# Expert weights of a mixture-of-experts layer: loads of 32 KB per partition, and the activations' transposition on VectorE

## What is computed

```python
    a = jnp.einsum('td,edf->tef', t, w_gate)      # 32 experts, w_gate and w_up (32, 2048, 512)
    u = jnp.einsum('td,edf->tef', t, w_up)
    act = jax.nn.silu(a) * u * combine[:, :, None]
    y = jnp.einsum('tef,efd->td', act, w_down)    # w_down (32, 512, 2048)
```

## Time and profile before

| what | value |
|---|---|
| time, median of 3 runs | 1390.5 us (1388.91 to 1390.74) |
| span of the profiled execution | 1388.4 us |
| PE busy | 1117.8 us, 81% |
| DVE, ACT busy | 545.0 us, 331.1 us |
| DMA, all queues | 481.20 MB, mean 347 GB/s |
| HBM read | 478.52 MB |

### The profile page before, as it was taken

One profiled execution on the slowest core, in us unless ns is written; L12 is line 12 of the kernel. 1 busy time (PEld: TensorE's weight loads), 2 busy tenths in 40 slices (PEclk: granted clock), 3 DMA queues, 4 the chain that ended last, 5 costly groups with the idle time before them and its releaser, 6 DMA issues.

```text
span 1388.4 us, 21683 instructions
## 1 busy us (share of the span) xinstructions
PE 1117.8 (81%) x8748; PEld 638.7 (46%) x8748; DVE 545.0 (39%) x1151; ACT 331.1 (24%) x611; POOL 33.2 (2%) x96
## 2 busy tenths in 40 slices
PE   8999999999999988677766667676766766767766
PEld 7888887878888633222222223222222222222222
DVE  5545576566665633332232232223232232222323
ACT  5654456665554210000000000000000000000002
POOL 1000000110001000000000000000000000000001
PEclk9999999999999999988998889888889998889898
DMA  7866653226785999999999999999999999999997
GB/s 241 274 200 182 177 170 109 92 92 226 271 291 172 410 423 426 428 425 425 427 426 427 426 425 426 428 426 426 427 424 426 427 429 425 427 424 427 428 424 306
DMA packets 93623, 481.20 MB, mean 347 GB/s; under 512 B 11719, under 2 KB 22093, under 8 KB 61454
## 3 DMA queue, kind: packets, MB, share of 16 engines
q1 hardware_dynamic: 93084, 478.22, 86.4%
q10 hardware_dynamic: 306, 2.11, 0.4%
q0 software_dynamic: 192, 0.31, 0.1%
HBM read 478.52 MB, written 2.10 MB: 346 GB/s over the span
## 4 chain that ended last, share of the span: by engine, by line
PE 47%; DMA 40%; ACT 5%; SPq 4%; DVE 3%; issue 2%; ACTq 0%; DVEq 0%
DMA gu<-in_w_up 40%; PE ps L588 7%; PE ps L590 7%; PE ps L589 7%; PE ps L1038 7%; PE ps L1093 5%; PE ps L1012 4%; SPq L424 3%; DVE w_lo L1603 1%; PE ps L1023 1%; SPq L434 1%; PE ps L555 1%; ACT x_slots L1509 1%; PE ps L816 1%; PE ps L818 1%
## 5 line engine op out<-in xcount | busy, mean ns | idle before, releaser
L1038 PE MATMUL ps<-gu,xe 128*32 128x256 f32 x3968 | 301.8, 471 | 178.1 <-DMA gu<-in_w_up 178.1
L1038 PEld LDWEIGHTS ps<-gu,xe 128*32 128x32 f32 x3968 | 148.7, 134 | 351.1 <-DMA gu<-in_w_up 222.8
L2109 DVE TENSOR_TENSOR x_sum<-ps,x_sum 128x512 f32<-128x512 f32 x240 | 149.1, 684 | 325.4 <-PE ps L1050 325.4
L1603 DVE TENSOR_TENSOR w_lo<-w_raw,w_hi 128x1024 fp32r<-128x1024 f32 (+1 forms) x137 | 163.2, 1200 | 129.2 <-ACT w_hi L1213 126.1
L588 PE MATMUL ps<-w_hi,a_hi 128*128 128x512 f32 (+1 forms) x468 | 183.0, 391 | 0.0
L589 PE MATMUL ps<-w_lo,a_hi 128*128 128x512 f32 (+1 forms) x468 | 179.8, 384 | 0.0
L590 PE MATMUL ps<-w_hi,a_lo 128*128 128x512 f32 (+1 forms) x460 | 176.9, 385 | 0.0
L1213 ACT ACTIVATE w_hi<-w_raw 128x1024 fp32r<-128x1024 f32 (+1 forms) x137 | 141.1, 1039 | 129.3 <-PE ps L590 114.7
L1093 PE MATMUL ps<-down,turned 128*32 128x512 f32 x976 | 119.5, 633 | 24.4 <-ACT turned L1522 24.4
L1516 ACT ACTIVATE sg<-ps 128x128 f32<-128x128 f32 x31 | 8.6, 278 | 546.0 <-PE ps L1038 546.0
L1012 PE MATMUL ps<-x_res,hot 128*32 128x512 f32 x496 | 111.9, 1030 | 0.0
(11 more groups left out here) (337 smaller groups left out, 884.1 us busy)
## 6 DMA issues: line engine op xcount, KB each, us to landing
gu<-in_w_gate SPq DMA_DIRECT2D x60, 2048.0 KB, 29.7
gu<-in_w_up SPq DMA_DIRECT2D x59, 2048.0 KB, 34.3
down<-in_w_down SPq DMA_DIRECT2D x118, 1024.0 KB, 20.9
w_raw<-in_w_in SPq DMA_DIRECT2D x56, 512.0 KB, 3.8
w_raw<-in_w_out SPq DMA_DIRECT2D x32, 512.0 KB, 4.7
w_raw<-in_w_mem_kv SPq DMA_DIRECT2D x16, 512.0 KB, 4.1
down<-in_w_down SPq DMA_DIRECT2D x16, 512.0 KB, 11.8
gu<-in_w_up SPq DMA_DIRECT2D x7, 1024.0 KB, 12.7
```

The lines of the kernel that those rows point to most:

```text
L1038: mm = pe.matmul(ps[5][j * SLOTS:(j + 1) * SLOTS, 0:2 * P].rearrange("s (m f) -> s m f", m=2), xe[:, k, :], gu[side][:, b, :, kk, j * P:(j ...
L1603: ve.tensor_tensor(w_lo[:, u % RING, :, 0:n], w_raw[:, u % RING, :, 0:n], w_hi[:, u % RING, :, 0:n], ALU.subtract).then_inc(S("w_split"), 1)
L2109: ins = ve.tensor_tensor(x_sum[:, t, cols], ps[g][:, :], (x_res if first else x_sum)[:, t, cols], ALU.add)
```

## The change

Gate and up of an expert are each loaded by one DMA of 4 MB, a run of 32 KB for each partition, into `gu` laid out as gate or up, then all 16 slices. Down is one tile `down` of 32 KB a partition, loaded by one DMA of 4 MB: partition p holds rows 4p to 4p + 3 of the expert's down weights, which lie behind each other in HBM. `load_gate_up` waits once, for `gu_used1`; `load_down` waits once, for `down_used`, which PE counts up after the last matmul of `project_down`. PE waits once for all of an expert's gate and up before the first matmul of `gate_up`, and once for all of its down weights.

As the hidden features are now spread over partitions in fours, DVE writes `act` with the four features of a partition set 32 columns apart, and turns it with one transposition in blocks of 32 by 32 (`gate(n)`); PE's transposition of `act` and ACT's copy of it are gone, and `project_down` waits for `act_turned`. DVE waits for `down_used` of the expert before, since `act_t` is overwritten. `x_sum` and `down_first` move to the place of `down0`, and `down` takes the place of the old `x_sum` and `down1`.

At the start, expert 0's down weights all come early, and where its last rows came (L467) now comes the first half of expert 1's in one DMA of 2 MB with runs of 16 KB. Expert 3's gate is issued ahead of expert 2's down, its up behind it. The pieces of experts 0, 1 and 2 and those of the last expert keep their sizes.

```diff
-        gu = [place("gu0", [P, 2, 2, KD // 2, FE], offset=e_at),
-              place("gu1", [P, 2, 2, KD // 2, FE], offset=w_at)]
-        down0 = place("down0", [P, 2, D], offset=e_at + 4 * 16 * 1024)
-        down1 = place("down1", [P, 2, D], offset=a_lo_at)
+        gu = [place("gu0", [P, 2, KD, FE], offset=e_at),
+              place("gu1", [P, 2, KD, FE], offset=w_at)]
+        down = place("down", [P, NJ, D], offset=a_hi_at)
+        at[0] = max(at[0], e_at + 5 * 16 * 1024)
-        turned_6 = place("turned_6", [P, TT + 1, P], offset=mla_mask_at)
+        comb_t = place("comb_t", [P, TT, P], offset=mla_mask_at)
+        act_t = place("act_t", [P, P], offset=mla_mask_at + 1024)
-        comb_t, act_t = turned_6[:, 0:TT, :], turned_6[:, TT, :]
-
-        x_sum = place("x_sum", [P, TT, D], offset=a_hi_at)
-        down_first = place("down_first", [P, 2, D], offset=a_hi_at)
+        x_sum = place("x_sum", [P, TT, D], offset=e_at + 64 * 1024)
+        down_first = place("down_first", [P, 2, D], offset=e_at + 64 * 1024)
...
 
-            def load_gate_up(e, side, used=None, halves=(0, 1), sides=(0, 1)):
-
-                wg = w_gate[0, e].rearrange("(p k) f -> p (k f)", k=KD)
-                wu = w_up[0, e].rearrange("(p k) f -> p (k f)", k=KD)
-                half = KD // 2 * FE
-                for b in halves:
-                    if used is not None:
-                        sp.wait_ge(S(f"gu_used{b}"), used)
-                    for m in sides:
-                        w = (wg, wu)[m]
-                        sp.dma_start(gu[side][:, b, m].rearrange("p k f -> p (k f)"),
-                                     w[:, b * half:(b + 1) * half]).then_inc(
-                                         S(f"gu_loaded{side}{b}"), 16)
-
-            def load_down(e, used, halves=(0, 1)):
-                wd = w_down[0, e].rearrange("(j p) d -> p j d", p=P)
-                for b in halves:
-                    dst = (down0, down1)[b]
-                    sp.wait_ge(S(f"down_used{b}"), used)
-                    for jj in range(2):
-                        sp.dma_start(dst[:, jj, :], wd[:, 2 * b + jj, :]).then_inc(
-                            S(f"down_loaded{2 * b + jj}"), 16)
-
-            def load_first(m):
-
-                w = (w_gate, w_up)[m][0, 0].rearrange("(k p) f -> p k f", p=P)
-                sp.dma_start(gu[0][:, 0, m], w[:, 0:KD // 2, :]).then_inc(S("gu_loaded00"), 16)
+            def load_gate_up(e, side, used, sides=(0, 1)):
+
+                sp.wait_ge(S("gu_used1"), used)
+                for m in sides:
+                    w = (w_gate, w_up)[m][0, e].rearrange("(p k) f -> p (k f)", k=KD)
+                    sp.dma_start(gu[side][:, m].rearrange("p k f -> p (k f)"), w).then_inc(
+                        S(f"gu_loaded{side}"), 16)
+
+            def load_down(e, used, half=None):
+
+                wd = w_down[0, e].rearrange("(p j) d -> p (j d)", j=NJ)
+                cols = slice(0, NJ * D) if half is None else slice(half * 2 * D, (half + 1) * 2 * D)
+                if used is not None:
+                    sp.wait_ge(S("down_used"), used)
+                sp.dma_start(down[:, :, :].rearrange("p j d -> p (j d)")[:, cols], wd[:, cols]).then_inc(
+                    S("down_loaded"), 16)
+
...
             sp.wait_ge(S("rstd"), 7)
             sp.wait_ge(S("logits_summed"), 1)
-            for jj in range(2):
-                sp.dma_start(down_first[:, jj, :], w_down[0, 0, (2 + jj) * P:(3 + jj) * P, :]).then_inc(
-                    S(f"down_loaded{2 + jj}"), 16)
-            for n, (k0, k1) in enumerate(FIRST_PIECES):
+            load_down(1, None, half=0)
+            for n, (k0, k1) in enumerate(REFILL):
                 if k1 < KD // 2:
                     sp.wait_ge(S("first_used"), n + 1)
                 else:
-                    sp.wait_ge(S("gu_used0"), 1)
-                for m, w in enumerate((w_gate, w_up)):
-                    sp.dma_start(gu[0][:, 0, m, k0:k1, :].rearrange("p k f -> p (k f)"),
-                                 w[0, 2].rearrange("(p k) f -> p (k f)", k=KD)[:, k0 * FE:k1 * FE]
-                                 ).then_inc(S("gu_loaded00"), 16)
-            load_gate_up(2, 0, 1, halves=(1,))
-            load_down(1, 1, halves=(0,))
-            load_gate_up(AHEAD, AHEAD % 2, AHEAD - 1, halves=(0,))
+                    sp.wait_ge(S(f"gu_used{k1 // KD}"), 1)
+                for m in range(2):
+                    load_piece(2, m, k0, k1)
+            load_down(1, 1, half=1)
+            load_gate_up(AHEAD, AHEAD % 2, AHEAD - 1, sides=(0,))
             load_down(AHEAD - 1, AHEAD - 1)
-            load_gate_up(AHEAD, AHEAD % 2, AHEAD - 1, halves=(1,))
+            load_gate_up(AHEAD, AHEAD % 2, AHEAD - 1, sides=(1,))
             load_down(AHEAD, AHEAD)
...
             def gate_up(b, side, loads, first=False):
 
-                more = 0
-                if side == 0:
-                    more = 96 if b == 1 else 0 if first else 32 * (len(FIRST_PIECES) - 1)
-                else:
-                    more = 16 + 16 * b
-                pe.wait_ge(S(f"gu_loaded{side}{b}"), 32 * loads + more)
+                if b == 0:
+                    if first:
+                        pe.wait_ge(S("gu_loaded0"), FIRST_GU)
+                    elif side == 0:
+                        pe.wait_ge(S("gu_loaded0"), 32 * loads + FIRST_GU + 32 * len(REFILL) - 64)
+                    else:
+                        pe.wait_ge(S("gu_loaded1"), 32 * loads + SECOND_GU - 32)
...
@@ -1068,15 +1052,13 @@
                 gather(n + 1)
                 gather_turn(n + 1)
                 pe.wait_ge(S("comb_ready"), TT * (n + 1))
-                pe.wait_ge(S("act_ready"), n + 1)
                 if m is not None:
                     pe.wait_ge(S("bank6_copied"), n)
                 for t in range(TT):
                     mm = pe.transpose(ps[6][:, t * P:(t + 1) * P],
                                       comb[:, t].rearrange("p g s -> p (g s)"), ident[:, :])
-                pe.transpose(ps[6][:, TT * P:(TT + 1) * P], act[:, :], ident[:, :]).then_inc(
-                    S("bank6_turned"), 1)
-                pe.wait_ge(S("bank6_copied"), n + 1)
+                mm.then_inc(S("bank6_turned"), 1)
+                pe.wait_ge(S("act_turned"), n + 1)
                 if m is not None:
                     pe.wait_ge(S("y_copied"), n)
                 project_down(n, first=m is None)
...
             def project_down(n, first=False):
 
-                for b, w in enumerate((down0, down_first if first else down1)):
-                    for jj in range(2):
-                        j = 2 * b + jj
-                        pe.wait_ge(S(f"down_loaded{j}"), 48 if first and b else 16 * (n + 1) + 16)
-                        for g in range(NJ):
-                            mm = pe.matmul(ps[7][g * SLOTS:(g + 1) * SLOTS, :],
-                                           act_t[:, j * SLOTS:(j + 1) * SLOTS],
-                                           w[:, jj, g * UN:(g + 1) * UN],
-                                           start=(j == 0), stop=(j == NJ - 1))
-                    mm.then_inc(S(f"down_used{b}"), 1)
+                if first:
+                    pe.wait_ge(S("first_down_loaded"), 16 * 2 * NJ)
+                else:
+                    pe.wait_ge(S("down_loaded"), 16 * (n + 1))
+                for j in range(NJ):
+                    w = down_first if first and j < 2 else down
+                    for g in range(NJ):
+                        mm = pe.matmul(ps[7][g * SLOTS:(g + 1) * SLOTS, :],
+                                       act_t[:, j * SLOTS:(j + 1) * SLOTS],
+                                       w[:, j, g * UN:(g + 1) * UN],
+                                       start=(j == 0), stop=(j == NJ - 1))
+                mm.then_inc(S("down_used"), 1)
...
@@ -1518,10 +1499,9 @@
                 sc.wait_ge(S("bank6_turned"), n + 1)
                 if m is not None:
                     sc.wait_ge(S("combined"), TT * m + TT)
-                    sc.wait_ge(S("down_used1"), n)
-                sc.activation(turned_6[:, :, :], ps[6][:, 0:(TT + 1) * P].rearrange(
-                    "p (t a) -> p t a", t=TT + 1), ACT.Copy).then_inc(S("bank6_copied"), 1)
-                sc.wait_ge(S("down_used1"), n + 1)
+                sc.activation(comb_t[:, :, :], ps[6][:, 0:TT * P].rearrange(
+                    "p (t a) -> p t a", t=TT), ACT.Copy).then_inc(S("bank6_copied"), 1)
+                sc.wait_ge(S("down_used"), n + 1)
                 sc.activation(y_sb[:, :], ps[7][:, :], ACT.Copy).then_inc(S("y_copied"), 1)
...
+            by_j = act[:, :].rearrange("p (j q) -> p q j", j=NJ)
+
+            def gate(n):
+
+                ve.tensor_tensor(by_j, sg[:, :].rearrange("p (q j) -> p q j", j=NJ),
+                                 ps[5][:, P:2 * P].rearrange("p (q j) -> p q j", j=NJ),
+                                 ALU.mult).then_inc(S("act_ready"), 1)
```

(26 more changed lines are left out.)

82 lines of the change are left out of this document (38 added, 44 removed).

## The result

| | before | after |
|---|---|---|
| median of 4 runs each, us | 1390.62 (1388.91 to 1390.79) | 1378.79 (1378.63 to 1379.2) |
| span of the profiled execution, us | 1388.4 | 1376.6 |
| one expert in the loop, us | 29.52 | 29.14 |
| DMA, 610 to 1310 us, GB/s | 426 | 432 |

The ratio of the times is 0.9917 [0.9903 to 0.9931]: 11.8 us less, where 10.3 were forecast.

What follows compares the result with a forecast made beforehand. The prediction took the DMA rate in the expert loop as the bound. 1388.4 - 10.4 (longer runs) + 0.3 (start) - 0.2 (end) = 1378.1 us, and 2.1 us more for the median: 1380.2 us, range 1376 to 1387.

Steps and rivals of the forecast that it cites:

- The rate: Expert loop: runs of 32 KB save 0.14 us (gate and up) and 0.22 us (down) an expert, 10.4 us together.
- The rival of 16 KB: Loads: a run of 32 KB moves as two of 16 KB did, giving 1386.0 us; chance 0.13.
- The slack: Expert loop: `down` is released 20.5 us after the landing, 7 us before it is needed, so the waits cost nothing.
- The limit: Expert loop: SP must have the release of `down` by 27.5 us after the landing, or the queue runs dry.
- The price of an overrun: Expert loop: each us by which `down` is released too late costs 29 us over the experts.
- The rival of the dry queue: Expert loop: with TensorE's clock low throughout, `down` is released late; 1 us over gives 1409 us; chance 0.04.
- The start: Start of the expert loop: later issues with less queued cost 0 to 4 us, 0.3 taken.
- VectorE's turn: `gate` to `project_down`: transposing the activations on VectorE takes 0.9 us an expert off PE's chain, hidden by the transfers.
- The end: Last expert: PE starts 1.3 us late but at full clock, -0.8 to +1 us, -0.2 taken.
- The sum: Whole kernel: the terms for loads, start and end, -10.4, +0.3 and -0.2 us, give 1378.1 us for the profiled execution.
- One sign: Profile slices: none from 451 us on was to stand below 410 GB/s.

Runs made afterwards that it cites:

- e2: e1 with gate, and with up, of an expert in one DMA of 4 MB, runs still 16 KB: 1390.08 us, 29.53 us an expert.
- e4: The changed kernel with down read in the old row order, runs of 8 KB, still one DMA: 1385.51 us, 29.37 us an expert.
- e3: The changed kernel with each 4 MB load cut into two DMAs of 2 MB, runs of 16 KB: 1384.82 us, 29.37 us an expert.
- e7: The changed kernel with `gather` done three times in each expert, 7 us more PE work: 1411.5 us, 29.6 us an expert in the mean.
- e8: The changed kernel with `gather` done four times in each expert, 10.5 us more PE work: 1429.7 us, 29.6 us an expert in the mean.
- e5: The changed kernel itself, run again beside other experiments: 1379.07 us, ratio 0.9921.
- e9: The changed kernel itself, run once more beside other experiments: 1378.72 us, ratio 0.9916.
- e11: The changed kernel with `gather` done twice in each expert, 3.5 us more PE work: 1386.87 us, 29.14 us an expert.
- e1: The kernel before with its own loads, but the coarse waits of the change on PE and SP: 1390.41 us, ratio 1.0008.

## Why the prediction was right, step by step

**The rate.** The term was 0.36 us an expert in the loop (0.14 for gate and up, 0.22 for down), from a packet of 1214.8 ns. Measured: 0.384 us and 1214.1 ns. The three steps it rests on held apart from one another: the run moves as one packet (the large packets' size above), the cost is on the run and not on the DMA (e2, and e4 with one DMA), and it is the same at each doubling (e3, e4). e3 and e4 were forecast at 29.36 us an expert by it, and took 29.37. The rival of 16 KB is what e3 is, 1384.8 us; it falls for the changed kernel. The Trainium skill's 3 cycles a packet ("DMA: Bandwidth & Descriptors", section "Why small descriptors are slow (HBM only)"), 3.5 ns by its clock, are about a third of what all three sizes here show. Its warning of rows a large power of two apart ("Latency and other measured facts") has no counterpart: down's rows now lie 32 KB apart and the loads are the fastest of all.

**The slack.** The release was forecast 20.5 us behind the landing and came at 19.2 (759.92 - 740.75). To `gather` it took 751.08 - 740.75 = 10.3 us (10.0 forecast), from there to `project_down` 5.1 (5.2). The term that was off is `project_down` itself, 3.7 us and not 5.3: the clock is up again by then. The limit was mis-sized the other way. I had put it at 27.5 us, with 1.7 us from an issue to its data moving, by the store in the earlier trace rows. In e7 releases at 23.8 us were on time and one at 25.1 was 0.7 us late, so that this distance was 4 to 5.3 us there; e8, at 27.3, loses little, which would fit the 27.5. The slack that the runs show to be safe is 23.8 - 19.2 = 4.6 us, not 7, and 3.9 us behind the latest release of 19.9. The price of an overrun, 29 us for each us, was at the high side: e8 is 3.5 us beyond 23.8 and loses 0.5 us an expert in the mean, not 3.5.

The rival of the dry queue rested on a misread row. The x16 of 736 to 737 us in the earlier trace rows counts every matmul that is under way in the window, also those that begin before it; the timeline of the same window has sixteen as one group that begins at 735.53 and lasts 1.93 us. At the lower clock, in the trace of before, four matmuls of `gate_up` begin every 0.42 us (735.12, 735.54, 735.96, 736.38), so that 128 take 13.6 us and not 8.0, and the release would come at some 33 us by the rival's own sum, far past its limit and not just short of it. It didn't happen because the clock was down for only some 5 us of PE's work in an expert (0.50 from 740 to 745 us, 1.00 from 746 us on), not because there was room for a clock that stays down.

**The start.** 0.3 us was taken out of 0 to 4. From the first `gate_up` to expert 4's landing the shorter loads should save 2 x 0.22 + 2 x 0.14 + 0.15 = 0.87 us and 0.29 were seen, so the start cost some 0.6; e5 and e9, the same kernel, took 90.59 and 90.14 us against 90.31, which makes it 0.4 to 0.9 against the one trace of before. One sum was slightly off: the 8 MB queued from 512.92 on are 9.94 + 9.79 = 19.7 us and not 19.6, which leaves the conclusion. The start is the thin place that the prediction took it for: e11's pads cost 5 us there and nothing in the loop.

**VectorE's turn.** Product and transposition take 0.43 and 0.31 us, and the turned activations are ready at 752.50, 3.7 us before `project_down` at 756.22: hidden, as said. The product's strided result cost 0.14 us over the earlier trace rows.

**The end.** -0.2 was forecast and -0.38 came. PE's three pieces of the last expert's `gate_up` and its `project_down`, of after, beside the earlier trace rows:

```profile
1344.87 3.66 PE L1094 MATMUL ps<-gu,xe 128*32 128x256 f32 x64
...
1353.65 1.93 PE L1094 MATMUL ps<-gu,xe 128*32 128x256 f32 x32
...
1357.43 1.92 PE L1109 MATMUL ps<-down,act_t 128*32 128x512 f32 x16
```

The first starts 21.3 us behind expert 30's landing (19.8 before), late from work as foreseen, and takes 3.66 us in place of 5.35. The third starts 30.1 us behind it, 30.3 before. The first comes 0.5 us later than the 20.8 forecast; that the total came out near is in part luck.

**The sum.** -10.4, +0.3 and -0.2 were -10.3; the change's own three lines measured -10.7. The rate gave 0.6 us more than forecast in the 26 experts of the table (9.99 against 26 x 0.36 = 9.4), and the start gave back about half of that, so the closeness of the two sums is in part luck; the mechanism is not. The 1.1 us that remain of the profiled difference lie ahead of the loop and come and go with the run. One sign was missed: a slice of 395 GB/s where none below 410 was to stand. It spans 447 to 482 us. The slice's edges don't explain it, as before moved 409 GB/s in the same stretch. Most of the difference lies from 463 to 474 us, ahead of the loop: 357 GB/s against 401. With the same loads there e9 has 360 and e11 390, and with the old ones e2 has 375 and e1 392. Why is open.

## What to carry to other kernels

Where DMA is the bound, take the time of a packet at two run lengths from the trace, extend the line, and price a longer run by it: here some 9.6 ns a run, whatever number of DMAs carries them, and 32 KB is the longest run that a 4 MB weight over 128 partitions has. Before you merge buffers or waits to get there, measure how far behind its data the release comes and where it must be: in a steady loop 3.5 us more work an expert was free, while at the loop's start, with an engine that hardly pauses, such delays added up from expert to expert and cost 5 us in the first four. Here a release 5.3 us ahead of the moment its data had to move was in time to 0.2 us, and one 4 us ahead not always, where a small store had suggested 1.7.

## What had not been expected of the hardware

The granted clock paid for part of PE's added work. Over the span it was 0.927 before and 0.909 in e1, whose coarse waits give PE one long pause an expert for two short ones; and then 0.905, 0.936, 0.966 and 0.996 for the changed kernel, e11, e7 and e8. With 10.5 us more work an expert, PE is busy for 94% of e8's span.

What a DMA queue costs that is filled late varied from 0 to 2.3 us between experts of one run with about the same lateness, and the rate stays uneven for some us behind it (459, 262, 311 GB/s in e7). What is lost shows in the packet records as packets of 1.3 to 2.9 us in place of 1.215, of which the changed kernel has none between 700 and 900 us. Why one kernel's experts differ so wasn't settled. Nor was the delay at the start tried apart from the one in the loop, by a pad on the first experts alone.
